# Experts' weights in runs of 8 KB, in a transformer kernel of three blocks

## The reference

```python
scores = jax.nn.sigmoid((t @ router_w).astype(jnp.float32))
...
for e in range(N_EXPERTS):
    he = jax.nn.silu(t @ w_gate[e]) * (t @ w_up[e])
    out = out + gates[:, e:e + 1] * (he @ w_down[e])
```

## Time and profile before

| | before |
|---|---|
| median of three executions | 1218.46 us |
| their range | 1216.21 to 1221.91 us |
| the profiled execution's own time | 1217.9 us |
| its span, first to last instruction | 1216.1 us |
| TensorE matmul busy | 1106.9 us, 91% |
| DMA | 356.14 MB, mean 293 GB/s |
| q1 (SP) | 147056 packets, 295.81 MB |
| q0 (POOL) | 17024 packets, 59.26 MB |
| first experts' stage, first product to last down product | 616.6 to 831.5 us |
| second | 990.3 to 1204.3 us |

### The profile page before, as it was taken

How to read it: one execution, slowest core, us unless ns; L and a number is a source line. 1 busy time by engine, 2 the same in 40 slices (tenths; PEclk the granted TensorE clock), 3 DMA queues, 4 the chain that set the end, 5 groups by cost and what they waited for, 6 DMA issues and landing times.

```text
span 1216.1 us, 17412 instructions
## 1 busy us (share of the span) xinstructions
PE 1106.9 (91%) x6792; PEld 742.0 (61%) x6792; DVE 593.3 (49%) x1175; ACT 432.2 (36%) x738; POOL 94.5 (8%) x189
## 2 busy tenths in 40 slices
PE   6999787989999999988999999887999999999986
PEld 6878444779999977855744343325887754343422
DVE  3588352566666656747513322226765532232223
ACT  6445321464445555536412010104546441020100
POOL 0201232320000000022000000002000000000000
PEclk9999989999999999998999999999999999999998
DMA  9956699698777744693679999997675479999995
GB/s 300 259 189 210 216 350 368 186 368 249 212 231 229 226 130 173 220 356 142 273 285 409 409 409 409 408 409 246 226 280 222 149 282 410 409 408 410 409 409 225
DMA packets 164174, 356.14 MB, mean 293 GB/s; under 512 B 10616, under 2 KB 79480, under 8 KB 163968
## 3 DMA queue, kind: packets, MB, share of 16 engines
q1 hardware_dynamic: 147056, 295.81, 66.8%
q0 software_dynamic: 17024, 59.26, 13.9%
q10 hardware_dynamic: 16, 0.02, 0.0%
HBM read 351.89 MB, written 7.36 MB: 295 GB/s over the span
## 4 chain that ended last, share of the span: by engine, by line
PE 69%; DMA 16%; DVE 9%; ACT 4%; issue 2%; POOL 0%; SPq 0%; ACTq 0%; DVEq 0%; POOLq 0%
PE bank L572 36%; PE bank L1124 12%; PE bank L1134 8%; DMA ering<-in_ada_w 4%; DMA ering<-in_moe_w_up 3%; DMA work<-in_moe_w_up 3%; DMA a_raw<-in_moe_w_up 3%; PE bank L1093 3%; PE bank L517 2%; DVE wlo L562 2%; DMA work<-in_ada_w 1%; DMA wraw<-in_w_up 1%; PE bank L731 1%; ACT whi L556 1%; PE bank L844 1%
## 5 line engine op out<-in xcount | busy, mean ns | idle before, releaser
L562 DVE TENSOR_TENSOR wlo<-wraw,whi 128x1024 fp32r<-128x1024 f32 x150 | 179.3, 1221 | 63.5 <-ACT whi L556 62.2
L556 ACT ACTIVATE whi<-wraw 128x1024 fp32r<-128x1024 f32 x150 | 153.8, 1054 | 53.2 <-PE bank L572 41.6
L572 PE MATMUL bank<-a_hi,whi 128*128 128x256 f32 x512 | 147.7, 289 | 1.3 <-DVE a_lo L761 1.1
L572 PE MATMUL bank<-a_lo,whi 128*128 128x256 f32 x512 | 146.2, 285 | 0.0
L572 PE MATMUL bank<-a_hi,wlo 128*128 128x256 f32 x512 | 146.1, 285 | 0.0
L1124 PE MATMUL bank<-ering,work 128*64 128x512 f32 x576 | 129.6, 595 | 9.9 <-DMA ering<-in_moe_w_up 5.6
L1324 DVE TENSOR_TENSOR work<-work,bank 128x512 f32<-128x512 f32 x16 | 11.0, 687 | 204.6 <-PE bank L1124 204.6
L572 PE MATMUL bank<-whi,a_hi 128*128 128x512 f32 x256 | 101.6, 397 | 5.8 <-DVE a_lo L761 3.0
L572 PEld LDWEIGHTS bank<-a_hi,whi 128*128 128x128 f32 x512 | 99.5, 194 | 8.4 <-issue 6.4
L1232 ACT ACTIVATE o_hi<-work 128x512 fp32r<-128x512 f32 x32 | 20.2, 631 | 236.8 <-DVE work L1292 236.3
L572 PE MATMUL bank<-whi,a_lo 128*128 128x512 f32 x256 | 99.9, 390 | 0.0
(11 more groups left out here) (324 smaller groups left out, 1856.8 us busy)
## 6 DMA issues: line engine op xcount, KB each, us to landing
ering<-in_moe_w_up SPq DMA_DIRECT2D x36, 1024.0 KB, 18.4
ering<-in_moe_w_down SPq DMA_DIRECT2D x36, 1024.0 KB, 18.1
ering<-in_moe_w_gate SPq DMA_DIRECT2D x36, 1024.0 KB, 17.4
ering<-in_ada_w POOLq DMA_DIRECT2D x52, 512.0 KB, 5.8
wraw<-in_w_in SPq DMA_DIRECT2D x28, 512.0 KB, 7.3
wraw<-in_a_w_qkv SPq DMA_DIRECT2D x24, 512.0 KB, 4.5
work<-in_moe_w_down SPq DMA_DIRECT2D x12, 1024.0 KB, 18.9
work<-in_moe_w_gate SPq DMA_DIRECT2D x12, 1024.0 KB, 15.8
```

Of the source, the lines that this page charges most:

```text
L556: nc.scalar.activation(w_hi(c), wraw[:, c % RING, :], ACT.Copy).then_inc(w_hi_done, 1)
L562: nc.vector.tensor_tensor(w_lo(u[0]), wraw[:, u[0] % RING, :], w_hi(u[0]).bitcast(F32), ALU.subtract).then_inc(w_lo_done, 1)
L572: mm = nc.tensor.matmul(out_ap, l, r, start=first and n == 0, stop=last and n == len(terms) - 1)
```

## The change

Each load holds half a matrix of one expert: for gate and up 512 rows of 512 numbers, four rows to a partition, for down 256 rows of 1024, two to a partition. That is one run of 8 KB for a partition. The loads of a pair keep their number and their places; two in a row are the same half for the first and the second expert. TensorE waits for both, does the products of a half (16 records of L1124 or L1134) and raises `e_used` by 2. The split place takes two DMAs with pieces of 4 KB of the one expert.

With four rows to a partition, a chunk of columns is every fourth one of a block of 512. The high and low normalised rows are now written in the order of the chunks, with two instructions of 512 elements for each former one of 1024, which read x with a step of four numbers and write runs. The gathering then reads runs; the router's transposes read x with a step of four (before two), and the transposes of the hidden values read with a step of two (before runs). The branch for experts with more than 64 tokens changes in the same way. The host's layout of vectors follows.

```diff
         def norm_split_hi(act, n, t):
             act.wait_ge(nrm_inv, n + 1)
-            nc.scalar.activation(hn_hi[:, t, :], x[:, t, :], ACT.Copy, scale=sm[:, M_RS + t:M_RS + t + 1]
-                                 ).then_inc(hn_done, 1)
+            for h in range(2):
+                part = slice(h * HALF, (h + 1) * HALF)
+                ins = nc.scalar.activation(by_chunks(hn_hi[:, t, part]), in_chunks(x[:, t, part]), ACT.Copy,
+                                           scale=sm[:, M_RS + t:M_RS + t + 1])
+            ins.then_inc(hn_done, 1)
...
+        def in_chunks(rows):
+            return rows.rearrange("p (q k) -> p k q", k=4)
+
+        def by_chunks(rows):
+            return rows.rearrange("p (k q) -> p k q", k=4)
...
         def pair_cols(k):
-            return slice(2 * P * (k // 2) + k % 2, 2 * P * (k // 2 + 1), 2)
+            return slice(HALF * (k // 4) + k % 4, HALF * (k // 4 + 1), 4)
...
         def pair_up(pe, r, bank, x_e, first, last):
-            m = r % LOADS
-            for kk in range(2):
-                k = 2 * (m % 4) + kk
+            half = r % LOADS % 4 // 2
+            for k in range(4):
                 for e in range(2):
                     rows = slice(PAIR_SLOTS * e, PAIR_SLOTS * (e + 1))
-                    mm = nc.tensor.matmul(bank[rows, :], x_e[:, k, rows], eunit(r, e)[:, kk * HALF:(kk + 1) * HALF],
-                                          start=first and kk == 0, stop=last and kk == 1)
+                    mm = nc.tensor.matmul(bank[rows, :], x_e[:, 4 * half + k, rows],
+                                          eunit(r + e, k // 2)[:, (k % 2) * HALF:(k % 2 + 1) * HALF],
+                                          start=first and k == 0, stop=last and k == 3)
             return mm
...
-                for j in range(4):
-                    m = 4 * kind + j
-                    r = LOADS * p + m
-                    pe.wait_ge(e_in[r % PLACES], eturn(l, r))
+                for half in range(2):
+                    r = LOADS * p + 4 * kind + 2 * half
+                    for e in range(2):
+                        pe.wait_ge(e_in[(r + e) % PLACES], eturn(l, r + e))
                     if kind == 0 and p % 2 == 0:
-                        pe.wait_ge(e_x, 4 * quad_of(l, p) + j + 1)
-                    pair_up(pe, r, psum[kind], xe[:, p % 2, :, :], j == 0, j == 3).then_inc(e_used, 1)
+                        pe.wait_ge(e_x, 4 * quad_of(l, p) + 2 * half + 2)
+                    pair_up(pe, r, psum[kind], xe[:, p % 2, :, :], half == 0, half == 1).then_inc(e_used, 2)
...
-                tr = nc.tensor.transpose(psum[2][:, k * P:(k + 1) * P], hid[:, k * P:(k + 1) * P], ident)
+                tr = nc.tensor.transpose(psum[2][:, k * P:(k + 1) * P], hid_cols(k), ident)
...
+                    e, half = 2 * p + m % 2, m % 4 // 2
                     if m < 8:
                         w = a["moe_w_gate_2" if m < 4 else "moe_w_up_2"][l]
-                        src = w[2 * p:2 * p + 2, 2 * P * (m % 4):2 * P * (m % 4 + 1), :].rearrange(
-                            "e (p k) n -> p e (k n)", k=2)
+                        src = w[e, HALF * half:HALF * (half + 1), :].rearrange("(p h k) n -> p h (k n)", h=2, k=2)
                     else:
-                        src = a["moe_w_down_2"][l][2 * p:2 * p + 2, P * (m % 4):P * (m % 4 + 1), :].rearrange(
-                            "e p n -> p e n")
+                        src = a["moe_w_down_2"][l][e, S * half:S * (half + 1), :].rearrange("(p h) n -> p h n", h=2)
```

More of the change, by code:

```diff
@@ L674, in norm_rows @@
                                      ).then_inc(hn_done, 1)
+        def in_chunks(rows):
+            return rows.rearrange("p (q k) -> p k q", k=4)
+        def by_chunks(rows):
+            return rows.rearrange("p (k q) -> p k q", k=4)
         def norm_split_hi(act, n, t):
             act.wait_ge(nrm_inv, n + 1)
-            nc.scalar.activation(hn_hi[:, t, :], x[:, t, :], ACT.Copy, scale=sm[:, M_RS + t:M_RS + t + 1]
-                                 ).then_inc(hn_done, 1)
+            for h in range(2):
[3 more added lines that the diff above has]
+            ins.then_inc(hn_done, 1)
         def norm_split_lo(dve, n, t):
             dve.wait_ge(hn_done, 2 * n - 1 + t)
-            nc.vector.scalar_tensor_tensor(out=hn_lo[:, t, :], in0=x[:, t, :], scalar=sm[:, M_RS + t:M_RS + t + 1],
-                                           in1=hn_hi[:, t, :].bitcast(F32), op0=ALU.mult, op1=ALU.subtract)
+            for h in range(2):
+                part = slice(h * HALF, (h + 1) * HALF)
+                nc.vector.scalar_tensor_tensor(out=by_chunks(hn_lo[:, t, part]), in0=in_chunks(x[:, t, part]),
+                                               scalar=sm[:, M_RS + t:M_RS + t + 1],
+                                               in1=by_chunks(hn_hi[:, t, part].bitcast(F32)), op0=ALU.mult,
+                                               op1=ALU.subtract)
         def norm_act(act, n, xs, last=False):
@@ L1117, in pair_up, with hid_cols @@
         def pair_up(pe, r, bank, x_e, first, last):
-            m = r % LOADS
-            for kk in range(2):
-                k = 2 * (m % 4) + kk
+            half = r % LOADS % 4 // 2
+            for k in range(4):
                 for e in range(2):
                     rows = slice(PAIR_SLOTS * e, PAIR_SLOTS * (e + 1))
-                    mm = nc.tensor.matmul(bank[rows, :], x_e[:, k, rows], eunit(r, e)[:, kk * HALF:(kk + 1) * HALF],
-                                          start=first and kk == 0, stop=last and kk == 1)
+                    mm = nc.tensor.matmul(bank[rows, :], x_e[:, 4 * half + k, rows],
+                                          eunit(r + e, k // 2)[:, (k % 2) * HALF:(k % 2 + 1) * HALF],
+                                          start=first and k == 0, stop=last and k == 3)
             return mm
         def pair_down(pe, r, first, last):
-            m = r % LOADS
-            for half in range(2):
-                for e in range(2):
-                    rows = slice(PAIR_SLOTS * e, PAIR_SLOTS * (e + 1))
-                    mm = nc.tensor.matmul(psum[4 + half][rows, :], hid_t[:, m % 4, rows],
-                                          eunit(r, e)[:, half * HALF:(half + 1) * HALF], start=first, stop=last)
-            return mm
+            half = r % LOADS % 4 // 2
+            for k in range(2):
+                for cols in range(2):
+                    for e in range(2):
+                        rows = slice(PAIR_SLOTS * e, PAIR_SLOTS * (e + 1))
+                        mm = nc.tensor.matmul(psum[4 + cols][rows, :], hid_t[:, 2 * half + k, rows],
+                                              eunit(r + e, k)[:, cols * HALF:(cols + 1) * HALF],
+                                              start=first and k == 0, stop=last and k == 1)
+            return mm
+        def hid_cols(k):
+            return hid[:, S * (k // 2) + k % 2:S * (k // 2 + 1):2]
         def scatter_bank(p, n):
@@ L1207, in pair_pe @@
                 pe.wait_ge(e_o, 2 * q)
-            for j in range(4):
-                r = LOADS * p + 8 + j
-                pe.wait_ge(e_in[r % PLACES], eturn(l, r))
-                pair_down(pe, r, j == 0, j == 3).then_inc(e_used, 1)
+            for half in range(2):
+                r = LOADS * p + 8 + 2 * half
+                for e in range(2):
+                    pe.wait_ge(e_in[(r + e) % PLACES], eturn(l, r + e))
+                pair_down(pe, r, half == 0, half == 1).then_inc(e_used, 2)
         def gathered_act(act, l, g):
@@ L1381, in over_pe @@
             pe.wait_ge(ov_in[l], ov(OV_IN, OV_IN, r, i))
-            for m in range(8):
-                mm = pair_up(pe, m, psum[m // 4], xe[:, 0, :, :], m % 4 == 0, m % 4 == 3)
+            for m in range(0, 8, 2):
+                mm = pair_up(pe, m, psum[m // 4], xe[:, 0, :, :], m % 4 == 0, m % 4 == 2)
             mm.then_inc(ov_pe[l], 1)
@@ L1392, in over_pe @@
             pe.wait_ge(ov_act[l], ov(OV_ACT, 3, r, i))
-            for j in range(4):
-                mm = pair_down(pe, 8 + j, j == 0, j == 3)
+            for half in range(2):
+                mm = pair_down(pe, 8 + 2 * half, half == 0, half == 1)
             mm.then_inc(ov_pe[l], 1)
@@ L2712, in pair_cols @@
     def pair_cols(v):
[L2714 removed]
+        return v.reshape(2, P, 4).transpose(1, 0, 2).reshape(P, KC)
     taps = lambda w: w.reshape(w.shape[0], -1, P).transpose(2, 1, 0).reshape(P, -1)
```

23 lines of the change are left out of this document (12 added, 11 removed).

## The result

The changed kernel is slower: 1229.08 us, median of four runs (1225.70 to 1229.91), against 1217.34 (1216.18 to 1221.91) for the kernel before on the same chip. The ratio, taken over all executions, is 1.0084 with a 95% interval of 1.0051 to 1.0117 (the two medians alone would give 1.0096). The forecast was 1216.4, with a range of 1211 to 1226. The profiled execution took 1229.91 us with a span of 1228.1; before it was 1217.9 and 1216.1.

What follows compares the result with a forecast made beforehand. After TensorE's first five pairs, the expert weight transfers at 409 GB/s set the pace. +3.4 start, +3.4 end, -11.4 stream, +0.5 split, +1.0 and +0.1 transposes, +1.2 ada = -1.8: 1216.1, median said 1216.4; range 1211 to 1226.

Steps and rivals of the forecast that it cites:

- norm split: Normalised rows before each expert stage: two instructions of 512 for one of 1024, +0.25 us; nothing for the 16 B step.
- The sum: All terms added, -1.8 us against the profiled execution's 1217.9, giving 1216.1; chance 0.50.
- Rival 2: Before each stage: a 16 B step doubles ACT, DVE and transpose time, 4.2 us a stage, 1224.8; chance 0.12.
- the router's transposes: Before each stage: their source step grows from 8 B to 16 B, +0.5 us a stage.
- The stream: Expert weight transfers: 8 KB packets instead of 4 KB gain 5.7 us a stage, plateau 422 GB/s instead of 409.
- The straight line: DMA packet times at 512 B, 2 KB and 4 KB lie on a line with a fixed part of 10 ns.
- Rivals 1 and 3: 1: 8 KB packets move no faster, 1228, chance 0.15; 3: some 2 us a stage gained, 1223, chance 0.07.
- rival 5: Better than the sum: ada not late, steps free, late stream start hidden, 1211; chance 0.10.
- Start and end of the stream: Each expert stage: first refill 1.7 us later, and sixteen records instead of eight after the last up load, 1.7 more.
- the sum's three stream terms: Both expert stages: +3.4 us for the start, +3.4 for the end, -11.4 for the stream.
- Rival 4: Bound part of the stages: the clock falls in longer waits, +3.4 us a stage, 1223; chance 0.06.
- The modulation's weights: First layer's attention: `ada_w` transfers get a third beside 8 KB expert packets; products late, +1.2 us carried to the stage.

Runs made afterwards that it cites:

- e6: The kernel before, its loads kept, with normalised rows written by chunks but read with a 16 B step (output of no use): 1224.61 us, ratio 1.0059.
- e7: The changed kernel with its step of four taken as two steps of two, in the row writing and in the gathering: 1220.68 us, ratio 1.0008.
- e5: The kernel before with only the down matrices loaded in 8 KB runs: 1219.17 us, ratio 1.0003.
- e8: e7 with the down loads and products of the kernel before, so only gate and up in 8 KB runs: 1220.19 us, ratio 1.0014.
- e10: e9 with twelve filler products of TensorE before the last scatter of each layer: 1214.79 us, ratio 0.9956.
- e1: The changed kernel with normalised rows written whole, without a step; the gathering reads with the 16 B step instead: 1227.92 us, ratio 1.0075.
- e3: The changed kernel with each load as two DMAs of 4 KB pieces, coarse grain kept: 1235.17 us, ratio 1.0140.
- e9: e7 with a layer's first four and last four gate or up loads in the old grain: 1217.06 us, ratio 0.9969.
- e11: The kernel before with only twelve filler products added before the last scatter of each layer: 1218.73 us, ratio 1.0010.
- e4: e1 with loads 5 to 10 of layer 0 in 4 KB pieces: 1227.13 us, ratio 1.0064.

## Why the prediction was wrong

**The step that failed** is in the norm split: "They also read x with a step of 16 B ... I take nothing." Between bounds of nothing and double time it chose the wrong end. Two `hn_hi` of 512 take 2.32 us (forecast 1.29), two `hn_lo` 2.21 (1.35), 1.8 and 1.6 times as long, on the path of both stages. e6 shows the step alone doing it, e7 the change without it.

It is the largest miss, not the only one. The sum said -1.8 us between the profiled executions, and their spans differ by +12.0. Of these 13.8 us, C and C2 are 6.7 (8.2 against 1.5 for split and transposes), E 2.1, D and D2 1.0, A and B 3.6 (4.8 against 1.2 for `ada_w`), and 0.4 stand elsewhere. With the first part alone the time would have been about 1223, inside the range. (The median said is also 0.3 too low: 1216.1 plus 0.6 is 1216.7.)

**Rival 2 had the place and the size, not all of the make-up.** It gave 4.2 us a stage, 1224.8. C and C2 lost 3.3 and 4.9, 8.2 together against 8.4. But its share for the router's transposes does not exist: sixteen take 2.56 us with a step of 16 B and 2.55 with 8, so the +0.5 a stage of the sum is gone too. Nor does its 0.75 beyond the cover: `sel` is ready at 618.3 and the gathering starts at 620.1, behind the fillers. What took their place is the clock. ScalarE's share (+1.15) and VectorE's (+0.92) make TensorE's wait 2.92 us instead of 0.84, 2.1 more in either layer, 4.1 together. The other 4.1 us arise behind the wait. Behind it the products before the gathering run at 1.2 GHz, and in layer 1 the first seven gathering products too, where before all ran at 2.4 (0.21 us apart in the changed kernel's timeline, then 0.12; before, 0.12 from the second on). In layer 0 it is the other way round, six of them at 1.2 GHz where before it was thirteen, which gives 0.8 us back; so C loses 3.3 and C2 4.9:

```profile
999.17 0.41 PE L1108 MATMUL bank<-sel,hn_lo 128*128 128x256 f32 x1
999.38 0.41 PE L1108 MATMUL bank<-sel,hn_hi 128*128 128x256 f32 x1
...
1001.03 0.28 PE L1108 MATMUL bank<-sel,hn_hi 128*128 128x256 f32 x1
1001.15 0.28 PE L1108 MATMUL bank<-sel,hn_lo 128*128 128x256 f32 x1
```

The clock also goes with C and C2 lying anywhere from 16.8 to 18.8 in the kernels without a 16 B step: where the whole gathering runs at 2.4 GHz they are 16.8 to 17.2 (e5 and e8 in layer 0; all but e8 and e10 in layer 1), elsewhere 18.4 to 18.8.

The Trainium skill (Advanced Engine Details and Errata, "SBUF Cachelines") was cited for this rival: lines of 16 B, two hits wanted in each. By that rule ScalarE, VectorE and the transposes should all have slowed. This case's runs agree for the first two, and for TensorE's loads of the fp32r rows in e1 (330 against 204 ns), and differ for the transposes of fp32 rows (210 against 209).

**The stream** was right in mechanism and size: 420 GB/s for 422, and 5.1 (plateaus) to 5.9 us (e3) a stage for 5.7. The straight line through three packet sizes held for a fourth: two packets of 4 KB at 409 GB/s take 320 ns on an engine, one of 8 KB at 420 takes 312, so the second one's fixed part was 8 ns where the line said 10. Rivals 1 and 3 are out, and so is rival 5, which took the steps as free. The Trainium skill (DMA: Bandwidth & Descriptors, "Why small descriptors are slow") has 3 cycles a packet, by which the gain was estimated at 2 us a stage; the trace, with 5.1 to 5.9, does not agree.

**Start and end of the stream** were right in mechanism and, priced by e3 and the plateaus, within 0.6 us a stage: 3.0 to 4.0 for 3.4. (e9, which takes the coarse grain away there, gains only 1.9 to 2.1, so the size is open between these.) The first refill comes 3.69 us after the first product (forecast 3.45), and sixteen records follow the last landing.

```profile
628.39 0.33 SPq L1594 DMA_DIRECT2D he_raw<-in_moe_w_up  x1
```

D and D2 together thus win 3.6 us, where the sum's three stream terms give 4.6.

**After the stage** the forecast had nothing for E, and it lost 2.1. Before, the turn's transposes start when the row is ready on ScalarE. In the changed kernel that row is ready at 849.32, but TensorE still has the fillers ahead of them, cut by a second pause, and the transposes start at 851.42. First before, then changed:

```profile
838.67 4.35 PE L1101 MATMUL bank<-con 128*128 128x128 f32 x22 [2.22 <-issue]
843.23 1.97 PE L731 MATMUL bank<-con,hn 128*128 128x128 f32 x16 [0.21 <-ACT hn L673]
```

```profile
845.16 1.16 PE L1116 MATMUL bank<-con 128*128 128x128 f32 x8 [1.21 <-DVE x_res L1337]
848.17 1.15 ACT L673 ACTIVATE hn<-x_res,sm 128x1024 f32<-128x1024 f32 x1 [0.23 <-DVE sm L710]
848.48 3.15 PE L1116 MATMUL bank<-con 128*128 128x128 f32 x14 [2.16 <-issue]
851.42 3.01 PE L745 MATMUL bank<-con,hn 128*128 128x128 f32 x16
```

The low clock has a part in it: it covers six of the eight last scatter products (most take 0.63 us instead of 0.39) and the fourteen fillers. But the scatter's share does not decide E, as e1 and e8 show (under e10). Rival 4 had the clock in mind, but in the bound part, where windows keep it at 1.00; it fell outside.

Why the second pause falls among the fillers is not shown. The page calls such time "issue", that is, TensorE waited for nothing that the profile shows. The trace shows one 16 KB packet of queue q8, which the page calls instruction, at each of the two pauses (842.41 to 843.73 us, just ahead of the first, and 845.78 to 847.08, across the start of the second). The kernel before has one at its pause (836.28), but also one at 839.28, where the fillers run on. What the packets have to do with the pauses is not shown.

**The modulation's weights** were costed at 1.2 us. The sharing came as worked out, q1 with twice q0's bytes between 537 and 542 us, answering to the earlier trace rows, and so did the late products; that the delay is carried to the stage did not. The changed kernel enters the attention 3.3 us later, so its product at 545.19 is the one that stood at 539.72 before, without a wait, and the one at 550.20 that of 544.99:

```profile
q1 hardware_dynamic: 179, 1.34, 65.9%
q0 software_dynamic: 182, 0.68, 34.0%
...
545.19 1.06 PE L517 MATMUL bank<-a_raw,silc 128*32 128x512 f32 x8 [2.15 <-DMA a_raw<-in_ada_w]
550.20 1.07 PE L517 MATMUL bank<-a_raw,silc 128*32 128x512 f32 x8 [0.47 <-DMA a_raw<-in_ada_w]
```

```profile
539.72 1.06 PE L517 MATMUL bank<-a_raw,silc 128*32 128x512 f32 x8
```

Counted from the end of A, these two come 2.6 and 2.3 us late, and the next one 0.4, as much as those before them; the forecast had 1.5 for the second of the three and 1.2 for the last, carried on. B is still 2.0 us longer in the changed kernel. 1.1 are there when sixteen small products at the end of the attention start (568.10), and these take 3.55 us at 1.2 GHz instead of 1.89. In e1, e7, e8, e9 and e10, whose early gate and up loads have 8 KB packets too, B is only 0.2 to 1.1 longer than before; in e5, with 8 KB for the three early down loads alone, it is 1.9.

**What stays open.** C, C2 and E lose 10.3 us, D and D2 win 3.6: that is 6.7 of the 12.0 between the two profiled spans. 4.8 more lie in A and B, nearly all of it code that is the same. The executions' clocks bear on it without settling it. Over the 95 executions of the kernel before that are listed with e1 to e11, a mean granted clock lower by 0.01 goes with some 6 us more. The changed kernel's four executions have 0.968 to 0.973, and those 95 have 0.969 to 0.985. In A the level is 1.2 GHz for 27.3 us in the changed kernel and for 20.6 before, but e10 has 27.3 too with an A of 460.8. e7 gave back 8.4 us, a little more than its C and C2 show (7.5). Whether the change itself lowers the clock in A and B, or four executions happened to have it, no run separates.

## What to carry over

Bound an unseen access step by a run or by the dear end of its range when it stands on the path: 0 was no better founded than double, and it was the largest term missed. It did not decide everything: with the step made cheap (e7) the change still came out even, and only fine ends (e9) made it faster. A step of four fp32 columns can be taken as two steps of two in two operations that are there anyway. Coarser loads pay in the middle of a stream and cost at its ends, so keep the old grain for the loads that open the stage and for those whose landing closes it. When two profiles are compared product by product, count from a point that both have: at equal clock times they show different products.

## What the runs showed of the hardware

- ScalarE and VectorE read fp32 with a step of 8 B in 0.75 us for 512 columns (e7), and with 16 B in 1.22 and 1.13 (changed kernel).
- TensorE's weight loads differ at a step of 16 B by what is loaded: the gathering's fp32r rows take 330 ns instead of 204 with 8 B (e1), the fp32 rows of the router's transposes 210 instead of 209.
- 8 KB packets move 420 GB/s in a steady stream, 4 KB ones 409; the fixed part of a packet comes out at 8 to 10 ns from 512 B to 8 KB.
- Two DMA queues with 8 KB and 4 KB packets sent 179 and 182 of them in 5 us, 1.34 against 0.68 MB: the longer packets take the larger share.
- TensorE can pause for 2 us and more without any wait that the profile shows, and the place moves with the instructions ahead of it. A second such pause of 0.9 us or more among the fillers after the stage goes with E of 25.5 us or more (changed kernel, e1, e3, e4, e7, e9); with none, or one of 0.6 (e5), E is 24.2 or less.
